# Windowed attention with sinks: scores issued two pairs ahead, softmax steps done by pairs of blocks

## The reference, cut to what matters

```python
def windowed_gqa(h, w_qkv, w_o, sinks, cos, sin):
    q = apply_rope(q ...); k = apply_rope(k ...)
    ...
    s = jnp.where(mask, s, -inf)                 # |i-j| <= WINDOW
    m = jnp.maximum(jnp.max(s, axis=-1), sink)
    e = jnp.exp(s - m)
    pr = e / (jnp.sum(e, axis=-1) + jnp.exp(sink - m))
    o = einsum(pr, v)
    return o @ w_o
```

## Time and profile before

| | us |
|---|---|
| three runs | 1026.81, 1027.63, 1027.73 |
| median | 1027.63 |
| span of the profiled execution, first to last instruction | 1024.9 |
| PE busy | 1016.4 (99%) |
| DVE busy | 778.0 (76%) |
| ACT busy | 609.6 (59%) |

### The profile page before, as it was taken

One profiled execution on the slowest core, in us unless ns is written; L12 is line 12 of the kernel. 1 busy time (PEld: TensorE's weight loads), 2 busy tenths in 40 slices (PEclk: granted clock), 3 DMA queues, 4 the chain that ended last, 5 costly groups with the idle time before them and its releaser, 6 DMA issues.

```text
span 1024.9 us, 15566 instructions
## 1 busy us (share of the span) xinstructions
PE 1016.4 (99%) x5912; PEld 871.5 (85%) x5912; DVE 778.0 (76%) x1104; ACT 609.6 (59%) x936; POOL 41.4 (4%) x78
## 2 busy tenths in 40 slices
PE   9999999999999999999999999999999999999997
PEld 7877888888888877788888888999899978888886
DVE  7987678988887887869988887866667667656654
ACT  6677766665657668667656556734444655444442
POOL 1000010000000000000000000500000000000000
PEclk9999999999999999999999999999999999999999
DMA  8633445655655551536665646555553356565541
GB/s 313 224 139 123 127 164 194 217 185 184 204 168 179 178 174 43 185 124 206 206 204 167 202 164 205 183 188 165 157 172 124 125 184 206 190 213 171 188 140 42
DMA packets 114639, 177.42 MB, mean 173 GB/s; under 512 B 3419, under 2 KB 85652, under 8 KB 114580
## 3 DMA queue, kind: packets, MB, share of 16 engines
q1 hardware_dynamic: 113316, 173.74, 51.4%
q10 hardware_dynamic: 1264, 2.88, 0.7%
HBM read 175.56 MB, written 1.05 MB: 172 GB/s over the span
## 4 chain that ended last, share of the span: by engine, by line
PE 98%; DVE 1%; DMA 0%; issue 0%; ACT 0%; POOL 0%; POOLq 0%; ACTq 0%
PE ps L1950 94%; PE ps L2058 1%; PE ps L2470 1%; PE ps L2104 1%; DMA raw<-in_diff_w_qkv 0%; PE ps L2612 0%; PE ps L2222 0%; PE ps L2543 0%; DVE h L1913 0%; PE ps L2242 0%; DVE wlo L1249 0%; DVE pp L1918 0%; DVE xs L1299 0%; PE ps L2187 0%; DVE whi L1510 0%
## 5 line engine op out<-in xcount | busy, mean ns | idle before, releaser
L1232 DVE TENSOR_TENSOR wlo<-raw,whi 128x2048 fp32r<-128x2048 f32 x147 | 335.4, 2288 | 72.9 <-ACT whi L642 72.7
L1950 PE MATMUL ps<-xs,whi 128*128 128x512 f32 (+1 forms) x1536 | 336.3, 352 | 0.0
L642 ACT ACTIVATE whi<-raw 128x2048 fp32r<-128x2048 f32 x147 | 279.2, 1909 | 41.0 <-PE ps L1950 30.5
L1950 PEld LDWEIGHTS ps<-xs,whi 128*128 128x128 f32 x1536 | 267.4, 189 | 39.3 <-issue 2.1
L1950 PE MATMUL ps<-xs,wlo 128*128 128x256 f32 x1248 | 202.4, 283 | 0.0
L1950 PE MATMUL ps<-whi,xs 128*128 128x512 f32 (+1 forms) x576 | 181.7, 392 | 0.2 <-issue 0.2
L1950 PEld LDWEIGHTS ps<-xs,wlo 128*128 128x128 f32 x1248 | 175.2, 191 | 2.9
L1950 PEld LDWEIGHTS ps<-whi,xs 128*128 128x128 f32 x576 | 106.7, 188 | 23.3 <-issue 2.3
L1950 PE MATMUL ps<-whi,ohi 128*128 128x512 f32 (+1 forms) x370 | 125.4, 397 | 0.0
L1950 PE MATMUL ps<-whi,olo 128*128 128x512 f32 (+1 forms) x370 | 122.5, 389 | 0.0
L1950 PE MATMUL ps<-wlo,ohi 128*128 128x512 f32 (+1 forms) x370 | 122.3, 389 | 0.0
(11 more groups left out here) (192 smaller groups left out, 962.0 us busy)
## 6 DMA issues: line engine op xcount, KB each, us to landing
raw<-in_ffn_w_up SPq DMA_DIRECT2D x44, 1024.0 KB, 5.1
raw<-in_w_in SPq DMA_DIRECT2D x23, 1024.0 KB, 5.3
raw<-in_ffn_w_down SPq DMA_DIRECT2D x22, 1024.0 KB, 4.9
raw<-in_w_mlp_in SPq DMA_DIRECT2D x16, 1024.0 KB, 5.4
raw<-in_w_mlp_out SPq DMA_DIRECT2D x16, 1024.0 KB, 4.9
raw<-in_diff_w_qkv SPq DMA_DIRECT2D x11, 1024.0 KB, 5.3
raw<-in_ple_w_gate SPq DMA_DIRECT2D x8, 1024.0 KB, 4.9
raw<-in_swa_w_qkv SPq DMA_DIRECT2D x6, 1024.0 KB, 5.2
```

The costliest lines, as they stand in the source:

```text
L642: act.activation(whi[:, u % RING, :], raw[:, u % RAW, :], ACT.Copy).then_inc(hi_ready, 1)
L1232: dve.tensor_tensor(wlo[:, u % RING, :], raw[:, u % RAW, :], whi[:, u % RING, :].bitcast(F32), ALU.subtract).then_inc(lo_ready, 1)
L1950: return pe.matmul(o, l, r, start=start, stop=stop, skip_group_check=True)
```

## The change

Scores of pair 2 are issued before the loop, and inside iteration s the scores of pair s+4 stand directly before `pv1(s)`, where before those of pair s+2 stood between the two `probs_T1`. In the bank, the mask is now written first and the scores are added to it. The query transposes stand at the head of iterations 4 and 6. `swa_max` handles four heads with one reduction over both banks, and makes the argument of the sink's exponential as well; `sink_exp` is one instruction on four values; `swa_exp` and `swa_scale` handle four heads per call, in two alternating buffers `Es`. On ScalarE and VectorE the calls within an iteration stand in another order. Nothing else is changed. The core of the diff:

```diff
 def swa_exp(s):                                   # ScalarE
-    act.wait_ge(max_ready, S_AT["1"] + s + 1)
-    for j in range(2): ...
+    act.wait_ge(max_ready, S_AT["1"] + s + 2)
+    for n in range(4): ...
...
 def sink_exp(s):
+    act.wait_ge(sink_arg, s // 2 + 1)
+    v = sinkd[:, s:s + 2, :]
+    act.activation(v, v, ACT.Exp).then_inc(sinkexp_ready, 2)
...
-                for s in range(2):
+                for s in (0, 2):
                     swa_exp(s)
                     sink_exp(s)
                 for s in range(0, 2 * N_A, 2):
-                    more = s + 2 < 2 * N_A
-                    copy_T(ATs[:, 0].rearrange("p k c -> p (k c)"), ps[:, TB, :])
-                    if s == 6:
-                        ple_proj(1, 1)
-                    elif s != 4:
-                        split_half()
-                    copy_T(ATs[:, 1].rearrange("p k c -> p (k c)"), ps[:, TB, :])
-                    if more:
-                        for n in (s + 2, s + 3):
-                            swa_exp(n)
-                            sink_exp(n)
-                    else:
-                        split_half()
-                    swa_hi(s)
                     if s in (4, 6):
                         copy_qs(slice(4, 8), (s - 4) // 2)
                     if s == 4:
                         ple_proj(1, 0)
-                    if s == 2:
+                    if s == 6:
+                        ple_proj(1, 1)
+                    copy_T(ATs[:, 0].rearrange("p k c -> p (k c)"), ps[:, TB, :])
+                    if 2 <= s < 2 * N_A - 2:
+                        swa_exp(s + 2)
+                    copy_T(ATs[:, 1].rearrange("p k c -> p (k c)"), ps[:, TB, :])
+                    if 2 <= s < 2 * N_A - 2:
+                        sink_exp(s + 2)
+                    if s not in (4, 6):
                         split_half()
+                    if s in (2, 14):
+                        split_half()
+                    swa_hi(s)
...
 def swa_max(s):                                   # VectorE
+                    g, qt, _, i = SWA_BLOCKS[s]
+                    dve.wait_ge(s_ready, S_AT["1"] + s + 2)
+                    pair = nmax1[:, s:s + 2, :]
+                    settle(dve.tensor_reduce(pair, ps[:, 6:8, :].rearrange("p r (j c) -> p r j c", j=2), AX.X, ALU.max, negate=True))
+                    dve.tensor_tensor(pair, pair, nsink4[:, g, :, i:i + 2], ALU.min).then_inc(max_ready, 2)
+                    dve.wait_ge(max_ready, S_AT["1"] + s + 2)
+                    dve.tensor_tensor(sinkd[:, s:s + 2, :], pair, sink4[:, g, :, i:i + 2], ALU.add).then_inc(sink_arg, 1)
...
                 swa_max(0)
-                swa_max(1)
                 split_half()
                 swa_scale(0)
-                swa_scale(1)
+                swa_max(2)
                 split_half()
+                swa_scale(2)
                 for s in range(0, 2 * N_A, 2):
-                    more = s + 2 < 2 * N_A
-                    if more:
+                    if 2 <= s < 2 * N_A - 2:
                         swa_max(s + 2)
-                        swa_max(s + 3)
-                        if s == 0:
-                            rope_cos(6, 0, *q2)
-                        elif s == 4:
-                            rope_cos(6, 1, *q2)
-                            rope_sin(6, 1, *q2)
-                        else:
-                            split_half()
+                    if s:
+                        swa_lo(s - 2)
+                    if s in (0, 2):
+                        rope_mul(6, s // 2, *q2)
+                    else:
+                        split_half()
+                    if 2 <= s < 2 * N_A - 2:
                         swa_scale(s + 2)
-                        swa_scale(s + 3)
-                    else:
-                        split_half(2)
-                    if s == 0:
-                        rope_sin(6, 0, *q2)
-                        rope_add(6, 0, 8)
-                    if s == 4:
-                        rope_add(6, 1, 8)
-                    swa_lo(s)
-                    if s == 10:
+                    if s in (10, 14):
                         split_half()
+                swa_lo(2 * N_A - 2)
...
 def scores1(s):                                   # TensorE
+                    for r in range(2):
+                        mm(pair[r][:, :, c:c + P], identb[:, :], maskb[:, qt, :].unsqueeze(1).broadcast_to([P, 2, P]), True, False)
                     for j in range(2):
                         for r in range(2):
                             rows_ = slice(r * HD, (r + 1) * HD)
-                            mm(pair[r][:, j, :], qS[rows_, 4 * g + i + j, qt * P:(qt + 1) * P], kT[rows_, g, :], j == 0, False)
-                    for r in range(2):
-                        mm(pair[r][:, :, c:c + P], identb[:, :], maskb[:, qt, :].unsqueeze(1).broadcast_to([P, 2, P]), False, True)\
-                            .then_inc(s_ready, 1)
+                            ins = mm(pair[r][:, j, :], qS[rows_, 4 * g + i + j, qt * P:(qt + 1) * P], kT[rows_, g, :], False, True)
+                    ins.then_inc(s_ready, 2)
...
                 q1_piece(1, 1)
+                scores1(2)
                 for s in range(0, 2 * N_A - 2, 2):
-                    probs_T1(s)
-                    scores1(s + 2)
-                    probs_T1(s + 1)
-                    piece1(s)
-                    pv1(s)
                     if s in (4, 6):
                         qk_T(6, "1q1", (s - 4) // 2, flat_tiles((s - 4) // 2, 4))
-                    piece1(s + 1)
+                        piece1(s)
+                        probs_T1(s)
+                        piece1(s + 1)
+                        probs_T1(s + 1)
+                    else:
+                        probs_T1(s)
+                        piece1(s)
+                        probs_T1(s + 1)
+                        piece1(s + 1)
+                    if s + 4 < 2 * N_A:
+                        scores1(s + 4)
+                    pv1(s)
                 probs_T1(2 * N_A - 2)
```

More of the change, by code:

```diff
@@ L198, in three_layer_kernel @@
         ATs = region(9216, 1024, "p (b k c) -> p b k c", b=2, k=4)
+        Es = [region(first, 1024, "p (n c) -> p n c", n=4) for first in (8192, 2560)]
         junk = region(10240, P)
@@ L296, in three_layer_kernel @@
         scaled_e = sem("scaled_e")
+        sink_arg = sem("sink_arg")
         dil_scaled = sem("dil_scaled")
@@ L399, in three_layer_kernel @@
         for s in range(2 * N_A):
+            if s in (4, 6):
+                T_ORDER.append(f"1q1{s // 2 - 2}")
             T_ORDER.append(f"1A{s}")
-            if s in (5, 7):
-                T_ORDER.append(f"1q1{(s - 5) // 2}")
         for s, (pr, qt) in enumerate(SB_PAIRS):
```

40 lines of the change are left out of this document (17 added, 23 removed).

## The result

The changed kernel took 1036.66 to 1038.59 us in four runs, median 1037.99, against 1027.22 (1026.64 to 1027.73, four runs) for the kernel before on the same chip: ratio 1.0104, 95% interval 1.0092 to 1.0116. The direction was forecast, the size was not: +10.8 us where I had +5.9, and above the range's upper end of 1036.2. One base of mine was off as well: I had put the 2.7 us between the span of the profile before and the median down to what lies outside the first and last instruction. In each of these four runs that part is 1.8 (1037.77 for the profiled one, with a span of 1036.0), so if it was so before too, 0.9 of the 2.7 was a profiled execution faster than the median, and the like-for-like forecast is 1032.6.

The account below looks back on a forecast made before the run. PE, busy 99% of the span, was taken as the bound. -0.99 + 2.31 + 1.90 + 2.71 = +5.9 moved the span from 1024.9 to 1030.8; with 2.7 to the median, 1033.5 us, range 1030.4 to 1036.2.

Parts of the forecast that it names:

- PE's row of work, -0.99: From 369.07 to the transposes of block 14, PE's own steps in the new order get 0.99 us shorter.
- the turn charged in the middle: Scores directly before the product with v, six times: array turn charged a middle value; whole term bounded -1.9 to 0.0.
- The three waits, 2.31 + 1.90 + 2.71: PE waits at block 1 and `piece1(6)` for ScalarE's copies, at block 14 for VectorE's scaling: 2.3, 1.9, 2.7 us.
- The third: Transposes of block 14 wait 2.7 us for VectorE's scaled exponentials, since iteration 12 has no scores; bounds 2.1 to 3.3.
- Elsewhere there is cover: Outside the three waits PE isn't held: plain iteration's exponentials done at about 3.1, mask wants its bank at 3.70.
- My rival of a thin cover: Cover of 0.6 between exponentials and mask too thin: six iterations wait some 0.3 more, +1.8, 1035.3 us; chance 5%.
- The clock: PE's granted clock stays at 1.00 behind the new waits, so the forecast adds nothing for a fall.
- the rival that had one: PE's clock falls to half after a wait of 2 us or more, one iteration costs 6.1 more: 1039.6 us; chance 3%.
- The merging: Merged reductions, exponentials and sink terms relieve ScalarE and VectorE; hidden behind PE, counted 0.
- The first wait: Transposes of block 1 wait 2.3 us for ScalarE's first copy out of `TB`, behind the exponentials; bounds 2.0 to 2.7.

Follow-up runs that it names:

- the undisturbed order: Changed kernel with all five PE waits removed by reordering ScalarE's and VectorE's calls, PE's order kept; 1026.17 us, ratio 0.9990 to the kernel before.
- the merged kernel: Kernel before with groups of four and the mask first, scores still one pair ahead and between the two groups of transposes; 1030.94 us.
- both kernels with few activations: The undisturbed order plus 16 or 8 one-column ScalarE activations in iteration 8, ahead of its first copy out of `TB`; 1027.41 and 1026.80 us.

## Why the prediction was wrong, and where it was right

**PE's row of work, -0.99:** right. It measured -0.89 where nothing disturbs it, and the scores followed by the product with v need 2.09 together (415.52 less 413.43), 0.01 from 1.06 + 1.02 with the turn charged in the middle. A plain iteration was forecast at 6.10 and took 6.11.

**The three waits, 2.31 + 1.90 + 2.71:** right in place, releaser and size: 2.32, 1.91 and 2.81. The third is 0.1 longer because the scaled exponentials came 0.07 later and PE was 0.03 earlier than worked out. Taking them away one by one took their cost away.

**"Elsewhere there is cover":** this step failed, and cost 1.8. I worked out only the plain iteration, where two groups of transposes and a piece stand between the first transposes and the mask (3.70), and let it speak for all. In iterations 4 and 6 the pieces stand ahead of the transposes, and the mask directly behind the second group, so it is wanted 2.25 after the first (1.81 and 0.44), while the exponentials end at 3.1 as everywhere. 0.9 twice was to be had from the numbers on record; it measured 0.94 and 0.85. The order of PE in these two iterations was in the diff, in its own branch. My rival of a thin cover also said +1.8, but for 0.3 in each of six iterations; the four plain ones have no wait at all, so that its size fits is luck.

**The clock:** this step failed too, and cost 3.2. The forecast charged nothing for a fall; the rival that had one held 3%, and a fall is what happened, twice. It cost 1.65 behind block 1; behind block 14, the product with v follows at 5.35 (434.60 less 429.25) where the undisturbed order has 3.82, so 1.5 more. What failed is the evidence against it. The earlier trace rows show a clock of 1.00 for 4.5 us after PE's last matmul, and I took this as proof that an idle time of that length does no harm. The next 1.9 us of the same trace, which I didn't read, are

```profile
1023.00:1024.90 1.90, 0.00 (x0) 0.00 (x0) 0.00 (x0) 0.00 (x0) 0.00 (x0) 0.68 0.53 202
```

so the clock had fallen there too (at about 1023.7, 5.2 us behind PE's last matmul), only later than my window, and a fall that comes late hits the work that follows the wait: in the changed kernel it came 1.2 us after PE had gone on. I had also worked out one price, 6.1 us, for the whole rival, where the trace shows 1.6 per stretch; two such stretches with a chance of their own each would have put up to 3.2 us on top of the sum and of the range's upper end. The Trainium skill, TensorE: Matmul & The Clock Gate, HAM oscillation, describes kernels whose waits between groups of matmuls bring the clock down for the work behind them; the trace agrees, at 0.50 behind waits of 2.2 and 2.7, though the waits of its example are longer.

**Sum.** -0.9 + 7.0 + 1.8 + 3.2 = +11.1, against 11.1 between the two spans. Of the +5.2 that the forecast span missed, 1.8 is the unchecked cover, 3.2 the clock, and 0.1 each the third wait and PE's row. The median of the runs rose by 10.8.

**The merging:** it was said that relief on ScalarE and VectorE is worth nothing by itself. That held, and more: with the mask first and the scores one pair ahead it costs 3.6, and no wait on the scaling is left in the order that has the change's distance of two pairs. The Trainium skill, Perfetto Trace Analysis, Optimizing Scalar/DVE Operations, whose rule I had weighed and given little room, pointed this way; the 0.27 us waits of the merged kernel agree.

**What stays open.** What decides in a given run whether a wait of 2.3 to 2.7 us is followed by a stretch at half clock, and whether by a short or a long one, was not settled: the same wait of 2.67 gave none, a short one and, twice, a long one in the profiled runs of four kernels. The first wait, of 2.16, was followed by a stretch of 3.3 to 3.4 us in all three profiled kernels that had it. Not explained either are the 0.6 us that both kernels with few activations have over the undisturbed order.

## What to carry to other kernels

A check of cover must be made for every distinct order in the loop, above all the special iterations in a branch of their own, and a last-in-line producer moved ahead of a copy must be traced to whoever waits for that copy. Where PE is at 98% or more, price a new wait of 2 us and more with what the clock may add behind it, and with a spread, not as its idle time alone. When a reordering loses, read PE's list of waits before giving it up: here five places in two other engines' programs turned +10.8 into -1.2, with PE's order untouched.

## What the runs showed of the hardware

- The idle time that the list of waits gives is less than the wait costs. From start to start 2.16 cost 2.32, 0.27 cost 0.43, 2.67 cost 2.81, 0.79 cost 0.94, and 1.66 cost 1.91. The difference is what the row ahead overlaps the next one when nothing waits: a matmul of 512 columns is busy 0.39 and the next starts 0.23 behind it (0.16), a group of transposes 0.66 and 0.41 (0.25).
- A granted clock of 0.50 came behind single waits of 2.16, 2.67 and 3.26 us in an otherwise dense stretch, in some cases while PE was still idle and in others 0.3 to 1.4 us after it had gone on; another wait of 2.67 and one of 2.33 had none behind them, and behind waits of 1.66, 1.22 and less there was none in any profiled run. A stretch of 3.3 to 3.4 us cost 1.5 to 1.7, one of 6.8 cost 2.7 to 2.8.
- One-column activations on ScalarE start 0.09 to 0.10 apart (46 of them from 402.7 to 406.9) while each is busy 0.187. Their mean duration is no measure of what a row of them costs.
